# A two-layer encoder on one NeuronCore: score tiles in one run, the root of a head moved into the next head, and another order of the first transfers' work

## The reference

```python
h = gelu(x @ a_w_in); u, v = split(h)            # layer 0 begins with v = x @ the second half
...
q, k, v = split(x @ w_qkv)                       # 8 heads, 2 x 64 query/key columns, 128 value columns
logits = einsum('bqhjd,bkhjd->bhjqk', q * 64**-0.5, k)      # j = 0, 1
probs  = softmax(logits + bias[:, :, None])
attn   = probs[:, :, 0] - lam * probs[:, :, 1]
o      = einsum('bhqk,bkhe->bqhe', attn, v)
o      = o * rsqrt(mean(o * o) + 1e-5) * subln_g * (1 - lambda_init)
out    = o.reshape(...) @ w_out
```

## Time and profile before

| what | us |
|---|---|
| median of 3 runs | 1277.54 |
| lowest and highest of them | 1277.07, 1277.98 |
| the profiled execution | 1278.11 |
| its span, from the first to the last instruction | 1276.4 |

### The profile page before, as it was taken

The page is one execution under the profiler, slowest core; times in us unless marked ns, Lnnn a source line. Parts: engine busy times, 40 slices in busy tenths (PEclk is TensorE's granted clock), DMA queues, the critical chain, the costliest instruction groups (busy, mean ns, idle before and its releaser), DMA issues.

```text
span 1276.4 us, 15650 instructions
## 1 busy us (share of the span) xinstructions
PE 1266.2 (99%) x6091; PEld 1055.6 (83%) x6091; DVE 650.0 (51%) x890; ACT 459.3 (36%) x553; POOL 165.0 (13%) x159
## 2 busy tenths in 40 slices
PE   9999999999999999999999999999999999999997
PEld 7888888889888888888888877788988888888886
DVE  3637877356343434432372777775743334343346
ACT  3422333322232323322314588775143222232230
POOL 3001100040000000000224444453100000000001
PEclk9999999999999999999999999999999999999999
DMA  8434554250433232223522334334032323322221
GB/s 263 148 99 117 177 169 148 89 194 1 132 98 99 81 101 83 99 97 99 184 75 72 99 108 124 91 108 166 33 99 99 99 99 99 99 99 100 95 102 66
DMA packets 104653, 140.64 MB, mean 110 GB/s; under 512 B 9441, under 2 KB 81465, under 8 KB 104353
## 3 DMA queue, kind: packets, MB, share of 16 engines
q1 hardware_dynamic: 95024, 127.81, 31.1%
q0 software_dynamic: 9440, 12.11, 2.9%
q10 hardware_dynamic: 144, 0.13, 0.0%
HBM read 137.85 MB, written 10.52 MB: 116 GB/s over the span
## 4 chain that ended last, share of the span: by engine, by line
PE 98%; DVE 1%; ACT 0%; DMA 0%; issue 0%; POOL 0%; DVEq 0%; SPq 0%; POOLq 0%
PE bank L1259 31%; PE bank L1263 31%; PE bank L1262 31%; PE bank L1650 1%; PE bank L1504 1%; PE bank L1269 1%; PE bank L1402 1%; PE bank L1507 0%; DMA w_raw<-in_a_w_in_dram 0%; PE bank L1393 0%; DVE prob L1137 0%; DVE w_lo L873 0%; PE bank L1680 0%; PE bank L1679 0%; ACT w_hi L514 0%
## 5 line engine op out<-in xcount | busy, mean ns | idle before, releaser
L1259 PE MATMUL bank<-xt_hi,w_hi 128*128 128x512 f32 (+1 forms) x1008 | 380.8, 378 | 0.0
L1263 PE MATMUL bank<-xt_hi,w_lo 128*128 128x512 f32 (+1 forms) x1008 | 378.8, 376 | 0.0
L1262 PE MATMUL bank<-xt_lo,w_hi 128*128 128x512 f32 (+1 forms) x1008 | 378.7, 376 | 0.0
L763 DVE TENSOR_TENSOR w_lo<-w_raw,w_hi 128x2048 fp32r<-128x2048 f32 x79 | 180.8, 2289 | 184.6 <-ACT w_hi L468 158.3
L1259 PEld LDWEIGHTS bank<-xt_hi,w_hi 128*128 128x128 f32 x1008 | 189.7, 188 | 36.6 <-issue 3.0
L1263 PEld LDWEIGHTS bank<-xt_hi,w_lo 128*128 128x128 f32 x1008 | 189.7, 188 | 34.6
L1262 PEld LDWEIGHTS bank<-xt_lo,w_hi 128*128 128x128 f32 x1008 | 189.8, 188 | 33.6
L468 ACT CAST w_hi<-w_raw 128x2048 fp32r<-128x2048 f32 x53 | 101.3, 1913 | 185.6 <-PE bank L1259 184.6
L1259 PE MATMUL bank<-w_hi,s_hi 128*128 128x512 f32 x416 | 162.1, 390 | 0.0
L1262 PE MATMUL bank<-w_lo,s_hi 128*128 128x512 f32 x416 | 161.8, 389 | 0.0
L1263 PE MATMUL bank<-w_hi,s_lo 128*128 128x512 f32 x416 | 161.8, 389 | 0.0
(11 more groups left out here) (209 smaller groups left out, 1488.3 us busy)
## 6 DMA issues: line engine op xcount, KB each, us to landing
w_raw<-in_f_w_in_dram SPq DMA_DIRECT2D x44, 1024.0 KB, 5.1
w_raw<-in_f_w_down_dram SPq DMA_DIRECT2D x22, 1024.0 KB, 4.8
w_raw<-in_a_w_in_dram SPq DMA_DIRECT2D x14, 1024.0 KB, 6.8
bias_by_query_key<-bias_by_distance POOLq DMA_DIRECT2D x8, 1024.0 KB, 16.0
w_raw<-in_a_w_out_dram SPq DMA_DIRECT2D x8, 1024.0 KB, 7.0
w_raw<-in_b_w_qkv_dram SPq DMA_DIRECT2D x16, 512.0 KB, 4.8
bias_sb<-bias_by_query_key SPq DMA_DIRECT2D x32, 256.0 KB, 2.6
w_raw<-in_b_w_qkv_dram SPq DMA_DIRECT2D x4, 1024.0 KB, 5.3
```

The source lines that it names most:

```text
L763: dve.tensor_tensor(lo_of(u), w_raw[:, u % 2, :], hi_of(u), ALU.subtract).then_inc(w_lo_done, 1)
L1259: ins = pe.matmul(o, a_hi, b_hi, start=start, stop=False)
L1262: pe.matmul(o, a_hi, b_lo, start=False, stop=False)
L1263: return pe.matmul(o, a_lo, b_hi, start=False, stop=stop)
```

## The change

- The scores of a head are made in one run of four tiles, behind the query projection, for all heads but head 0. Tiles 2 and 3 go to banks 5, 6, 0 and 2; the key projection goes to bank 3, the squares to bank 4; the waits follow.
- `root` is split into `log` and the rest. `log(h - 1)`, `root(h - 1)` and `values(h - 1)` on VectorE run in turn h instead of turn h - 1.
- On VectorE all four `probs_lo` and the low query part come first, the mixes go behind the last scores, and `square_lo` goes to the end of the turn. On TensorE `mean_square` goes to the end of the turn.
- GpSimd makes the weight unit in one go and then the four shares.
- At the start the first x tile goes ahead of the first weight piece on ScalarE and VectorE, and eight constant products stand where three did.

```diff
         def query_key_bank(c):
-            return bank[2 * c]
-        def score_bank(t, j):
-            return bank[(1, 4)[j] if t % 2 else 2 + j]
+            return bank[3 * c]
+        def score_bank(h, t, j):
+            if h == 0:
+                return bank[(1, 4)[j] if t % 2 else 2 + j]
+            return bank[((2, 3), (1, 4), (5, 6), (0, 2))[t][j]]
         def pair_bank(n):
-            return bank[5 + n - TB if n < TB + 2 else 0]
-        def square_bank(h):
-            return bank[0 if h < H - 2 else 4]
+            return bank[5 + n - TB if n < TB + 2 else 3 * (n - TB - 2)]
+        def square_bank():
+            return bank[4]
...
-            for t in range(TB):
+            x_half(0, 0)
+            piece(0)
+            for t in range(1, TB):
                 piece(t)
                 x_half(t, 0)
             x_half(0, 1)
...
-            def root(h):
+            def log(h):
                 act_e.preload_act_table_set("natural_log")
                 act_e.wait_ge(ms_mm, h + 1)
                 if h >= 1:
                     act_e.wait_ge(o_done, h)
-                act_e.activation(o_rs[:, :], square_bank(h)[:, :], ACT.Ln, bias=eps_col[:, 0:1]).then_inc(ln_done, 1)
+                act_e.activation(o_rs[:, :], square_bank()[:, :], ACT.Ln, bias=eps_col[:, 0:1]).then_inc(ln_done, 1)
+            def root(h):
                 act_e.wait_ge(ln_done, h + 1)
                 act_e.activation(o_rs[:, :], o_rs[:, :], ACT.Exp, scale=-0.5).then_inc(rs_o_done, 1)
@@ -706,13 +713,14 @@
                 weights(U_QK1 + h + 2)
                 probs_hi(h, 2)
                 probs_hi(h, 3)
-                exps(h + 1, 0)
-                exps(h + 1, 1)
-                exps(h + 1, 2)
+                if h:
+                    log(h - 1)
+                query_key(h + 2, 0)
+                if h:
+                    root(h - 1)
+                for t in range(TB):
+                    exps(h + 1, t)
                 squares(h)
-                query_key(h + 2, 0)
-                exps(h + 1, 3)
-                root(h)
                 query_key(h + 2, 1)
             h = H - 2
             probs_hi(h, 0)
@@ -720,8 +728,10 @@
             weights(U_BO)
             probs_hi(h, 2)
             probs_hi(h, 3)
+            log(h - 1)
+            values_hi(TB + 2)
+            root(h - 1)
             exps(h + 1, 0)
...
             stationary(o_t, None, 1, o_done, 4)
+            log(h - 1)
             root(h - 1)
             probs_hi(h, 2)
             probs_hi(h, 3)
             weights(U_BO + 2)
             squares(h)
+            log(h)
             root(h)
             weights(U_BO + 3)
...
                 query_key(h + 1, 1)
-                probs_lo(h, 0)
-                probs_lo(h, 1)
-                probs_lo(h, 2)
+                for k in range(TB):
+                    probs_lo(h, k)
+                query_key(h + 2, 0)
                 scored(h + 1, 0)
-                probs_lo(h, 3)
                 scored(h + 1, 1)
+                if h:
+                    values(h - 1)
+                scored(h + 1, 2)
                 weighed(h + 1, 0)
+                scored(h + 1, 3)
                 weighed(h + 1, 1)
-                scored(h + 1, 2)
                 mixed(h + 1, 0)
-                scored(h + 1, 3)
                 mixed(h + 1, 1)
                 weighed(h + 1, 2)
-                square_lo(h)
-                query_key(h + 2, 0)
                 mixed(h + 1, 2)
                 weighed(h + 1, 3)
                 mixed(h + 1, 3)
-                values(h)
+                square_lo(h)
             h = H - 2
             query_key(h + 1, 1)
-            probs_lo(h, 0)
-            probs_lo(h, 1)
-            probs_lo(h, 2)
+            for k in range(TB):
+                probs_lo(h, k)
+            values_lo(TB + 2)
             scored(h + 1, 0)
-            probs_lo(h, 3)
             scored(h + 1, 1)
+            values(h - 1)
+            scored(h + 1, 2)
             weighed(h + 1, 0)
-            values_lo(TB + 2)
+            scored(h + 1, 3)
             weighed(h + 1, 1)
-            scored(h + 1, 2)
             mixed(h + 1, 0)
-            scored(h + 1, 3)
             stationary(o_t, S_BO, 0)
...
@@ -1434,7 +1446,7 @@
                 if n:
                     lows(n - 1)
                 else:
-                    constant_products(3)
+                    constant_products(8)
                 highs(n)
             turn_half(0, 1)
@@ -1590,13 +1602,13 @@
                     if c == 0:
                         unit_ready(u)
                     if h == 0:
-                        pe.wait_ge(bv_lo_done, 2 * c + 1)
+                        pe.wait_ge(bv_lo_done, 3 * c + 1)
                     elif c == 1:
-                        pe.wait_ge(sc_done, 2 * TB * (h - 1) + 5)
-                    elif h < 3:
+                        pe.wait_ge(sc_done, 2 * TB * (h - 1) + (6 if h == 1 else 2))
+                    else:
                         pe.wait_ge(qk_lo_done, 2 * h - 1)
-                    else:
-                        pe.wait_ge(ln_done, h - 2)
+                        if h >= 3:
+                            pe.wait_ge(sc_done, 2 * TB * (h - 1))
                 ins = blocks(query_key_bank(c), u, c, 2 * P, 0, S, frees, ks)
...
                         pe.wait_ge(qk_lo_done, 2 * H - 1)
-                        pe.wait_ge(ln_done, H - 2)
+                        pe.wait_ge(sc_done, 2 * TB * (H - 1))
                 if t == 2 and u == U_V67:
-                    pe.wait_ge(bv_lo_done, TB + 3)
+                    pe.wait_ge(sc_done, 2 * TB * (H - 1) + 2)
                 hi = w_hi[:, u % 2, :].rearrange("p (k n) -> p k n", n=2 * P)
...
                     if h == 0:
                         pe.wait_ge(bv_lo_done, TB)
+                    else:
+                        pe.wait_ge(sc_done, 2 * TB * h)
+                if t == 1 and h >= 2:
+                    pe.wait_ge(ln_done, h - 1)
+                if t == 2 and h:
+                    pe.wait_ge(at_lo_done, TB * h)
                 for j in range(2):
-                    n = 2 * TB * h + 2 * t + j
-                    if n >= 4:
-                        pe.wait_ge(sc_done, n - 3)
+                    if h == 0 and t >= 2:
+                        pe.wait_ge(sc_done, 2 * t + j - 3)
+                    elif t == 3 and j == 0:
+                        if h < H - 1:
+                            pe.wait_ge(qk_lo_done, 2 * h + 3)
+                        else:
+                            pe.wait_ge(bv_lo_done, TB + 3)
+                    elif t == 3:
+                        pe.wait_ge(sc_done, 2 * TB * h + 1)
                     r = slice(HD * j, HD * j + HD)
                     q = slice(t * P, t * P + P)
-                    product(score_bank(t, j)[:, :], qk_hi[r, h % 2, 0, q], qk_lo[r, h % 2, 0, q],
+                    product(score_bank(h, t, j)[:, :], qk_hi[r, h % 2, 0, q], qk_lo[r, h % 2, 0, q],
...
             def mean_square(h):
                 pe.wait_ge(sq_lo_done, h + 1)
-                if h < H - 2:
-                    pe.wait_ge(qk_lo_done, 2 * h + 5)
-                else:
-                    pe.wait_ge(sc_done, 2 * TB * H)
-                if h == H - 1:
+                pe.wait_ge(sc_done, 2 * TB * (h + 1) + 4 if h < H - 2 else 2 * TB * H)
+                if h:
                     pe.wait_ge(ln_done, h)
                 hi, lo = squares_of(h)
-                pe.matmul(square_bank(h)[:, :], ones[:, :], hi[:, :], start=True, stop=False)
-                pe.matmul(square_bank(h)[:, :], ones[:, :], lo[:, :], start=False, stop=True).then_inc(ms_mm, 1)
+                pe.matmul(square_bank()[:, :], ones[:, :], hi[:, :], start=True, stop=False)
+                pe.matmul(square_bank()[:, :], ones[:, :], lo[:, :], start=False, stop=True).then_inc(ms_mm, 1)
...
                 project(h + 2, 0, range(0, 3))
                 turn_probs(h, 2)
                 turn_probs(h, 3)
-                scores(h + 1, 0)
-                scores(h + 1, 1)
-                project(h + 2, 0, range(3, 6))
-                values(h, 0)
-                values(h, 1)
-                scores(h + 1, 2)
-                scores(h + 1, 3)
-                values(h, 2)
-                values(h, 3)
-                project(h + 2, 0, range(6, KD))
-                project(h + 2, 1, range(0, 4))
+                project(h + 2, 0, range(3, KD))
+                for t in range(TB):
+                    scores(h + 1, t)
+                project(h + 2, 1, range(0, 3))
+                for k in range(TB):
+                    values(h, k)
+                project(h + 2, 1, range(3, KD))
                 mean_square(h)
-                project(h + 2, 1, range(4, KD))
             h = H - 2
             turn_probs(h, 0, 1)
             turn_probs(h, 1)
             value_pair(U_V67, 0)
             turn_probs(h, 2)
             turn_probs(h, 3)
-            scores(h + 1, 0)
-            scores(h + 1, 1)
```

(33 more changed lines are left out.)

1 line of the change is left out of this document (removed).

## The result

Four runs of the changed kernel: **1291.06 us** median (1290.71 to 1293.51), the kernel before 1277.67 beside it. The ratio is 1.0109 (95% interval 1.0097 to 1.0122): slower, by 13.4 us where 9.5 were forecast, and 0.06 us outside the range. The profiled execution took 1291.09 us.

What follows compares the result with a forecast made beforehand. TensorE, busy 1266.2 of 1276.4 us, was taken as the bound, so a change loses where it makes TensorE wait. Loop 10.2 + last heads 0.7 - start 1.4 = plus 9.5 on 1277.54: 1287.0 us, range 1280.5 to 1291.

Steps and rivals of the forecast that it cites:

- Part 1: Scores of four tiles in a row, seven heads: one run's entry and exit go, saving about 0.42 us a turn.
- Part 2: VectorE's order in the loop: TensorE waits 2.2 us for the squares' low part; plus 1.81 a turn, 10.2 in six.
- the row chosen for share and mix: Loop, GpSimd's second share meeting VectorE's first mix: by the row at 791.09, mix plain 0.68, share stretched to 1.23 us.
- the 9.3 variant: Loop bound where GpSimd's second share holds the mix back, so the second mix starts at 15.95: plus 9.3 us.
- Rival (c): Clock falls in TensorE's new loop waits: 2.9 us a turn, 17 more, 1304 us; chance 0.03.
- my high bounds: The parts' upper ends added: 1277.54 + 13.2 + 1.2 - 0.1 = 1291.8 us.
- Part 3: Root moved into the next head: costs nothing beyond the 0.67 us on VectorE already counted in the loop.
- Part 4: GpSimd's unbroken weight unit ahead of the shares, and SyncE's weight load behind four bias loads: costs nothing.
- Part 5: Last two heads: the third value product waits for the last value pair's low part; plus 0.7 us, bounds minus 0.8, plus 1.2.
- Part 6: Start: first product 0.15 us earlier, clock rise 2.7 earlier through unbroken work; minus 1.4 us, bounds minus 0.1 and minus 1.9.

Runs made afterwards that it cites:

- the fastest kernel: Changed kernel with VectorE and ScalarE reordered, squares in PSUM, and SyncE loading query and key weights ahead of the biases: 1274.51 us against 1277.49.
- e3_pair_first: Changed kernel with the third tile pair of the last values ahead of the first two value products of head 6: 1292.02 us (ratio 1.011).
- e2_filled_wait: Changed kernel with eight extra products, their result overwritten, in TensorE's wait ahead of each mean square of the loop: 1289.03 us (ratio 1.009).
- e1_squares_hole: Changed kernel with the squares' low part one mix earlier on VectorE, between the third reciprocal and the third mix: 1282.12 us (ratio 1.0035).
- e8_new_order: Changed kernel with another order on VectorE and ScalarE and the squares in a free PSUM bank, TensorE's loop untouched: 1277.80 us against 1277.82.

## Why the prediction was right and wrong

- **Part 1** held: one run of 12 slots takes 3.00 us, forecast 2.98, and the fastest kernel shows the whole 0.38 to 0.39 a turn (19.49 to 19.10; forecast 0.42).
- **Part 2** held in its mechanism and nearly in size. With t counted from a turn's first transposes, TensorE reached the mean square at t = 18.66 (forecast 18.6), the first mix began at 14.90 (14.85), the fourth ended at 20.02 (20.2), the squares' low part at 20.62 (20.8). A turn grew by 1.73 to 1.77 us, forecast 1.81; six turns without the fall of the clock by 9.9, forecast 10.2. What failed is the row chosen for share and mix: the first mix, begun 0.08 behind the share of 795.28, was held to 1.16 us and the share ran its 0.70. That is the 9.3 variant, which the rule of SBUF — State Buffer, section "SBUF: two separate sides", of the Trainium skill gave. The sum came out nearer to 10.2, mainly because the next turn starts 0.63 behind the squares' low part, where I had 0.45.
- **Rival (c)**, the clock, is the step that put the result out of the range. I made it an all-or-nothing case at 2.9 us a turn with a chance of 0.03, and the sum held nothing for it. It came in two of seven waits, at some 1.6 us each: 3.2 of the 3.5 us by which the span missed. "Against it: no wait of 2 us in this trace lies in warm work" was absence of evidence; an unseen price belongs in the range. The range had a fault of its own: my high bounds added up to 1291.8, and I ended it at 1291.
- **Part 3** was right: in the changed kernel the moved root delays nothing (the scores run unbroken for 3.00 us). The kernel before with its squares last shows what it costs unmoved.
- **Part 4** was right for the changed kernel alone. "the unit is wanted after the next turn's transposes, now itself later. Nothing" names its cover, a turn of 21 us. At 19.1, and with the last score reduction later still, the cover is gone, and the late weights cost 2.8 us in the six turns (117.4 against 114.6).
- **Part 5**: plus 2.31, of which the clock 1.55. The remaining 0.76 matches the forecast of 0.7, but by luck. I missed that the first value product of head 6 now needs the output product of head 5, at 858.70 on VectorE, for bank 7; TensorE waited 1.6 there, and so came late enough for the low part that I had named. On the timelines of VectorE and TensorE:

```profile
858.70 0.75 DVE L1162 SCALAR_TENSOR_TENSOR o_t<-bank,sub_g,o_rs 128x512 f32<-128x512 f32 x1
```

```profile
859.55 0.47 PE L1271 MATMUL bank<-at_hi,val_hi 128*128 128x512 f32 x1 [1.58 <-issue]
```

- **Part 6** is not shown as a cause: minus 0.96 in the profile (forecast minus 1.4), with the rise at 10.1 as I had it, but no run ties it to the edit. One rise in one profile was all I had, and I took it for a consequence of unbroken work. Over the other profiles it comes at 10.7 and 10.9 with the old start, at 10.2 with x first and TensorE idle, and at 8.0 to 13.1 with eight constants. Most of the 0.96 is the late rise of the one profile before.

Open is why two of the seven waits were followed by a fall of the clock and the others not: the runs show that standing still is what it takes, not what picks the turn, and the mean clocks of the other runs suggest that the number changes from one to the next.

## What to carry to other kernels

Joining matmul runs saves what the sequence of slots says, 0.4 us a run here, only if the engine that feeds them has its list ordered by when each result is wanted: write that list with times, factors before reductions, and put what is wanted last, last. A cover named in a costing (a load that is hidden because the turn is longer) is a condition: when the next repair shortens the turn, look at every cover again, the transfers' order among them. And a new wait on a warm TensorE has a second price, the clock, that may come in some turns only.

## What the runs showed of the hardware

- Waits of 1.2 to 1.9 us in warm work were followed by a fall to 1.2 GHz in 2 of 7 cases in the changed kernel (granted clock 0.79 over 8 us). A 2.3 us wait did it in e3_pair_first, and in the kernel with its squares last one of six waits of up to 1.5. With products in the wait (e2_filled_wait), or with waits of 1.0 (e1_squares_hole), none fell, and the 1.6 us wait at the value product was followed by no fall in any of three profiles.
- Who gives way, VectorE or GpSimd, depended here on the form of VectorE's instruction, not on who began. A mix (two SBUF inputs and a factor) begun 0.08 behind a share took 1.16 and the share 0.70. A subtraction of two SBUF tiles begun 0.07 to 0.08 behind a share took its plain 0.68 and the share 1.23. In e1_squares_hole both pairs stand in one turn and each gives way in its own manner (mix 1.16 and share 0.70; subtraction 0.68 and share 1.23). The starts are those recorded, and GpSimd's are rough. With one input of the subtraction in PSUM both ran at their plain lengths (timelines of GpSimd and VectorE in e8_new_order):

```profile
794.12 0.70 POOL L1915 TENSOR_SCALAR prob<-prob,rsum 128x512 f32<-128x512 f32 x1 [1.63 <-DVE rsum L1146]
```

```profile
794.19 0.68 DVE L1174 TENSOR_TENSOR sq_lo<-bank,sq_hi 128x512 fp32r<-128x512 f32 x1
```

  SBUF — State Buffer, section "SBUF: two separate sides", of the Trainium skill says that the first to start holds the pair. The mixes agree; the subtractions, at 791.16, 795.95 and 834.82, don't.
